# Differential attention on one Trainium2 core: paired score matmuls, the mask through an fp32r identity, and negated scores whose minimum is the bias

## The reference, cut to what matters

```python
def diff_causal_attention(q, k, v, lam):
    # q,k: (B,H,2,S,64); v: (B,H,S,128); lam: scalar
    for j in range(S_ // Q_BLOCK):                    # 8 blocks of 128 queries
        lo, hi = j * Q_BLOCK, (j + 1) * Q_BLOCK
        s = jnp.einsum('bhmqd,bhmkd->bhmqk', q[:, :, :, lo:hi], k[:, :, :, :hi]) * 64 ** -0.5
        mask = jnp.arange(hi)[None, :] <= jnp.arange(lo, hi)[:, None]
        p = jax.nn.softmax(jnp.where(mask, s, -jnp.inf), axis=-1)
        pd = p[:, :, 0] - lam * p[:, :, 1]
        outs.append(jnp.einsum('bhqk,bhkd->bhqd', pd, v[:, :, :hi]))
    return jnp.concatenate(outs, axis=2)
```

## Time and profile before

| | us |
|---|---|
| median of 3 runs | 3958.72 |
| lowest, highest | 3958.52, 3963.06 |
| profiled execution | 3959.2 |
| its span | 3957.3 |
| differential attention in it (481.3 to 652.3) | 171.0 |
| mean granted TensorE clock, share of full | 0.932 |

### The profile page before, as it was taken

How to read it: one execution, slowest core, us unless ns; L and a number is a source line. 1 busy time by engine, 2 the same in 40 slices (tenths; PEclk the granted TensorE clock), 3 DMA queues, 4 the chain that set the end, 5 groups by cost and what they waited for, 6 DMA issues and landing times.

```text
span 3957.3 us, 39477 instructions
## 1 busy us (share of the span) xinstructions
PE 3490.5 (88%) x16470; PEld 2812.1 (71%) x16470; DVE 1314.1 (33%) x1746; ACT 691.2 (17%) x1040; POOL 1209.5 (31%) x1052
## 2 busy tenths in 40 slices
PE   5958998779969899899899999994975789999997
PEld 4657865668848678777688888883764568888886
DVE  4153065022150440222411121125699442222223
ACT  2210144121020540001100000002321211000011
POOL 3102201314413023233334343431441234443431
PEclk9978998889979899999999999996987789999998
DMA  2100100101221001012011111111000111111111
GB/s 111 43 16 27 43 1 22 53 13 52 96 91 43 12 22 64 32 43 85 32 54 43 53 42 53 42 53 59 33 22 21 64 43 43 53 42 53 42 53 42
DMA packets 32651, 179.60 MB, mean 45 GB/s; under 512 B 3728, under 2 KB 6800, under 8 KB 15632
## 3 DMA queue, kind: packets, MB, share of 16 engines
q1 hardware_dynamic: 18864, 137.37, 9.8%
q10 hardware_dynamic: 13664, 40.42, 2.7%
HBM read 163.10 MB, written 14.68 MB: 45 GB/s over the span
## 4 chain that ended last, share of the span: by engine, by line
PE 79%; DVE 15%; ACT 3%; issue 2%; POOL 1%; DMA 0%; DVEq 0%; ACTq 0%; POOLq 0%
PE ps L353 46%; PE ps L382 15%; PE ps L408 5%; DVE c_out L1848 4%; PE ps L1610 2%; PE ps L656 2%; DVE xlo L316 1%; PE ps L278 1%; PE ps L1278 1%; PE ps L1294 1%; PE ps L272 1%; DVE n_sq L310 1%; PE ps L718 1%; PE ps L676 1%; DVE n_acc L261 1%
## 5 line engine op out<-in xcount | busy, mean ns | idle before, releaser
L447 POOL TENSOR_TENSOR whi<-raw,par 128x512 fp32r<-128x512 f32 x131 | 146.8, 1121 | 2642.3 <-PE ps L353 1970.3
L451 POOL TENSOR_TENSOR wlo<-raw,whi 128x512 fp32r<-128x512 f32 x524 | 784.0, 1496 | 41.7
L353 PE MATMUL ps<-xhi,whi 128*128 128x512 f32 x2368 | 742.9, 395 | 49.8 <-DVE xlo L316 33.7
L353 PE MATMUL ps<-xlo,whi 128*128 128x512 f32 x2368 | 735.3, 392 | 0.0
L353 PE MATMUL ps<-xhi,wlo 128*128 128x512 f32 x2368 | 733.7, 391 | 0.0
L353 PEld LDWEIGHTS ps<-xhi,whi 128*128 128x128 f32 x2368 | 446.0, 190 | 160.7 <-issue 32.9
L353 PEld LDWEIGHTS ps<-xlo,whi 128*128 128x128 f32 x2368 | 449.3, 190 | 95.0
L353 PEld LDWEIGHTS ps<-xhi,wlo 128*128 128x128 f32 x2368 | 447.9, 189 | 94.3
L449 POOL CAST whi<-raw 128x512 fp32r<-128x512 f32 x393 | 300.1, 764 | 0.0
L382 PE MATMUL ps<-hidden_lo,whi 128*128 128x512 f32 x864 | 269.1, 393 | 0.0
L382 PE MATMUL ps<-hidden_hi,whi 128*128 128x512 f32 x864 | 268.5, 392 | 0.4 <-DVE hidden_lo L1165 0.4
(11 more groups left out here) (409 smaller groups left out, 4088.4 us busy)
## 6 DMA issues: line engine op xcount, KB each, us to landing
raw<-stream SPq DMA_DIRECT2D x131, 1024.0 KB, 4.7
h_scr<-h ACTq DMA_DIRECT2D x2, 4096.0 KB, 12.1
h<-h_scr ACTq DMA_DIRECT2D x2, 4096.0 KB, 14.9
x_in<-xT ACTq DMA_DIRECT2D x4, 1024.0 KB, 14.6
x_again<-xT ACTq DMA_DIRECT2D x4, 1024.0 KB, 8.0
outT<-h ACTq DMA_DIRECT2D x8, 512.0 KB, 3.0
bias<-bias ACTq DMA_DIRECT2D x1, 2560.0 KB, 18.8
o_scr<-o_staged ACTq DMA_DIRECT2D x2, 1024.0 KB, 5.8
```

The costliest lines, as they stand in the source:

```text
L353: mm = nc.tensor.matmul(ps[:, c0 + c:c0 + c + width], w, x(k, a, width), start=(n == 0 and m == 0), stop=(n == len(ks) - 1 and m == 2))
L447: nc.gpsimd.tensor_tensor(WHI[:, r, t], RAW[:, r, t], one, ALU.mult).then_inc(hi_done, 1)
L451: ins = nc.gpsimd.tensor_tensor(WLO[:, r, t], RAW[:, r, t], WHI[:, r, t].bitcast(F32), ALU.subtract)
```

## The change

The two maps' score matmuls are issued in turn, chunk by chunk, on the two halves of the rows, and both masks come after them. All of it waits once, for both exponentials of the step before. The mask matmul takes fp32r copies of identity and mask, made once by ScalarE in the place of `w_if`, which is no longer needed. Queries are scaled by -1/8 when they are copied, and the mask is negated: PSUM holds negated scores, their minimum is the bias of the exponential, and its scale is -1. Two small products of the combination become one instruction. The buffer of squares is single.

```diff
+            pe.wait_ge(S("mask_ready"), 2)
             for i in range(n_steps + 2):
                 if i < n_steps:
                     h, j = STEPS[i]
+                    n = P * (j + 1)
+                    wait(pe, S("d_exp"), 2 * i)
+                    for c in range(0, n, HALF):
+                        w = min(HALF, n - c)
+                        for m in range(2):
+                            rows = slice(64 * m, 64 * m + 64)
+                            nc.tensor.matmul(ps[:, 2 * BANK * m + c:2 * BANK * m + c + w], QT[rows, h, P * j:P * (j + 1)],
+                                             KD[rows, h, c:c + w], start=True, stop=c + w < n)
                     for m in range(2):
-                        wait(pe, S("d_exp"), 2 * i + m - 1)
-                        rows = slice(64 * m, 64 * m + 64)
-                        n = P * (j + 1)
-                        for c in range(0, n, HALF):
-                            w = min(HALF, n - c)
-                            diag = c + w == n
-                            mm = nc.tensor.matmul(ps[:, 2 * BANK * m + c:2 * BANK * m + c + w], QT[rows, h, P * j:P * (j + 1)],
-                                                  KD[rows, h, c:c + w], start=True, stop=not diag)
-                            if diag:
-                                e = 2 * BANK * m + n - P
-                                mm = nc.tensor.matmul(ps[:, e:e + P], IDENT, par("mask_qk", 0, P), start=False, stop=True)
-                        mm.then_inc(S("d_scores"), 1)
+                        e = 2 * BANK * m + n - P
+                        nc.tensor.matmul(ps[:, e:e + P], IDR[:, :], MKR[:, :], start=False, stop=True).then_inc(S("d_scores"), 1)
...
+            nc.scalar.activation(IDR[:, :], IDENT, ACT.Copy).then_inc(S("mask_ready"), 1)
+            nc.scalar.activation(MKR[:, :], par("mask_qk", 0, P), ACT.Copy, scale=-1.0).then_inc(S("mask_ready"), 1)
+            for name, dst, scale in (("q_d", QT, -SCD), ("k_d", KD, 1.0)):
...
-                                             bias=SM[:, i % 4, 2 + m:3 + m], scale=SCD,
+                                             bias=SM[:, i % 4, 2 + m:3 + m], scale=-1.0,
...
-                    v.step(nc_v.tensor_scalar(SM[:, s % 4, 0:1], SM[:, s % 4, 4:5], LM[:, 2:3], None, ALU.mult))
                     v.wait()
-                    v.step(nc_v.tensor_scalar(SM[:, s % 4, 1:2], SM[:, s % 4, 0:1], SM[:, s % 4, 7:8], None, ALU.mult))
+                    v.step(nc_v.scalar_tensor_tensor(SM[:, s % 4, 1:2], SM[:, s % 4, 4:5], LM[:, 2:3], SM[:, s % 4, 7:8],
+                                                     ALU.mult, ALU.mult))
...
-                        v.step(nc_v.tensor_reduce(SM[:, i % 4, m:m + 1], ps[:, 2 * BANK * m:2 * BANK * m + n], AX, ALU.max))
-                        v.wait()
-                        nc_v.tensor_scalar(SM[:, i % 4, 2 + m:3 + m], SM[:, i % 4, m:m + 1], -SCD, None, ALU.mult)\
+                        nc_v.tensor_reduce(SM[:, i % 4, 2 + m:3 + m], ps[:, 2 * BANK * m:2 * BANK * m + n], AX, ALU.min)\
                             .then_inc(S("d_nm"), 1)
```

More of the change, by code:

```diff
@@ L506, in build @@
             PTD = [at("p_t0", A + 84992, [P, 896]), at("p_t1", A + 80896, [P, T])]
-            OSQ = at("o_squares", X + 65536, [P, 2, P])
+            OSQ = at("o_squares", X + 65536, [P, P])
+            WIF_AT = C + -(-4 * PARAMS["w_if"][0] // 32) * 32
+            IDR = at("identity_r", WIF_AT, [P, P], F32R)
+            MKR = at("mask_r", WIF_AT + 4 * P, [P, P], F32R)
             KM = at("k_mem", A + 49152, [P, H1, MEM])
@@ L799, in act_block1 @@
             act.wait_ge(S("ht_ready"), 2 * H1)
-            for name, dst in (("q_d", QT), ("k_d", KD)):
+            nc.scalar.activation(IDR[:, :], IDENT, ACT.Copy).then_inc(S("mask_ready"), 1)
+            nc.scalar.activation(MKR[:, :], par("mask_qk", 0, P), ACT.Copy, scale=-1.0).then_inc(S("mask_ready"), 1)
+            for name, dst, scale in (("q_d", QT, -SCD), ("k_d", KD, 1.0)):
                 q0 = WH[name][1]
@@ L804, in act_block1 @@
                     act.wait_ge(quad_ready, q + 1)
-                    nc.scalar.activation(dst[:, b, :], half(q, b % 2), ACT.Copy).then_inc(free(q), 1)
+                    nc.scalar.activation(dst[:, b, :], half(q, b % 2), ACT.Copy, scale=scale).then_inc(free(q), 1)
             q0 = WH["v_d"][1]
@@ L831, in act_block1 @@
                     act.wait_ge(S("d_on"), s + 1)
-                    wait(act, S("d_sq"), s - 1)
-                    nc.scalar.activation(OSQ[:, s % 2, :], QT[:, h, P * j:P * (j + 1)], ACT.Square,
+                    wait(act, S("d_sq"), s)
+                    nc.scalar.activation(OSQ[:, :], QT[:, h, P * j:P * (j + 1)], ACT.Square,
                                          accum_out=OS1[:, 0, s:s + 1]).then_inc(S("d_sq"), 1)
```

## The result

| | before | changed |
|---|---|---|
| median, us | 3958.62 | 3934.35 |
| lowest, highest | 3957.56, 3963.06 | 3933.24, 3937.59 |
| runs | 4 | 4 |
| ratio, 95% interval | | 0.9939, 0.9927 to 0.9951 |
| span of the profiled execution | 3957.3 | 3935.7 |

24.3 us faster.

What follows compares the result with a forecast made beforehand. TensorE was taken as the bound, with the whole change in one stage. Gains by head of 10.3 + 3.5 + 3.5 + 5.5 = 22.8 us, less 7 for clock falls, gave 16: 3943 us, range 3935 to 3953.

Steps and rivals of the forecast that it cites:

- What bounds the kernel now: Edited stage, 171.0 us: holds the whole gain or loss; TensorE never waits in its widest step of 6.77 us.
- Scores in turn on two row halves: Score matmuls: a pair of maps costs what one map cost, 0.20 + 0.213k us for k key blocks.
- Rival 4: Score matmuls: the halves do not run together, each step grows by 0.213k, total 3964 to 3990 us; chance 0.03.
- rival 3: Edited stage: the clock stays at 1.2 GHz, 25 us slower, 3984 us; chance 0.06.
- Mask through fp32r: Mask matmuls: 0.11 us each, where two took 0.75 a step with their changes of tile.
- VectorE: Small operations: 64 of 0.154 us go, and 0.46 of 0.56 us is left ahead of each combination.
- The new wait: Both maps wait for both exponentials: a step is 1.28 + 0.588k us, a full-clock head gains 3.5.
- The tiling rule, weighed: Whole stage: TensorE alone would save 12 us a head, some 50 in all; the loop leaves 3.5 a head.
- Head 1, at 1.2 GHz: First head: loop of 1.5 + 0.80k us, clock back at step 5; 45.8 to 35.5 us, gain 10.3.
- Head 4 with tail: Last head and tail: 48.2 to about 42.7 us, gain 5.5, of which 3.5 is the head.
- What the clock takes back: Starts of heads 2 to 4: four to six clock falls of 1.0 to 1.7 us, 7 us; bounds 0 and 13.
- Rival 1: Edited stage: the clock is held and the loop alone sets the time, 3936 us; chance 0.15.

## Why the prediction missed

**What bounds the kernel now**: right. TensorE left no time in a wide step before; the stage held the whole change.

**Scores in turn on two row halves**: right. A pair at k = 8 took 1.92 us (priced 1.90), at k = 1 0.42 (priced 0.41). Rival 4 is out. So is rival 3: the clock is at 1.2 GHz for 17 of the stage's 148.8 us.

**Mask through fp32r**: right, somewhat low. Two masks took 0.27 us to the transposes (priced 0.22), and the reader started 0.36 after the mask (priced 0.31). In fp32 a step is 0.16 longer (0.1 in the text).

**VectorE** and **Copies**: right. 0.45 from reciprocal to combination (priced 0.46).

**The new wait**: right, but for one leg, and the core of the case. Measured 3.65, 4.22, 4.78, 5.34, 5.93 for k = 4 to 8, against 3.63, 4.22, 4.81, 5.40, 5.99. The leg that differs: the chain goes through one minimum and both exponentials, not through two minima and the second exponential. Both paths are ready within 0.03 us of each other in wide steps (618.26 + 1.11 and 617.00 + 2.36), so the forecast of a step came out right although the path was the other one; that is luck in the sizes of the two operations. Steps 1 to 3 measured 4.36, 3.28, 3.10 (4.3, 3.2, 3.3). A head at full clock is 34.65, a gain of 4.0 where 3.5 was priced.

**The tiling rule, weighed**: by TensorE's work alone a head would have lost 12 us. TensorE's busy time did fall by 12.0 (37.5 to 25.5), the head by 4.0. The Trainium skill, TensorEngine Tiling (Array Packing), section Performance Considerations, has it that tiling does not quicken the reading of PSUM. The trace agrees: a minimum over 1024 columns takes 1.22 us as the maximum did, the exponential 1.11 as before, and 20 us of extra TensorE work cost nothing.

**Head 1, at 1.2 GHz**: right. 2.83, 3.20, 3.98, 4.75, then 4.22, 4.78, 5.35, 5.93: 35.0 (priced 35.5). The clock rose 14.3 us in, at the step named.

**Head 4 with tail**: too low. From the same end points 48.16 went to 41.73, a gain of 6.4 where 5.5 was priced. 0.4 is the head; the rest is a fall that the kernel before had in its tail (645.7 to 649.1) and the changed kernel has not. The 0.96 of the earlier trace rows showed it, and the sum left it out. There is one trace of the kernel before, so it stays open whether that fall is in all of its runs.

**What the clock takes back**: this is the step that failed. Its place was right: the only fall stands at the start of a head, and costs 1.5 us, inside the 1.0 to 1.7 named. The count was wrong: one, not four to six, so 1.5 us instead of 7. It came from the mean clocks of two other stages, with the new one put between them by its busy share. That share does not tell the count: heads 2 and 3 of the changed kernel run the same instructions in the same steps, and one fell and the other did not. The kernel with the fp32 mask has a busier TensorE (28.9 of 37.3 us in head 3, against 27.1 of 36.1, each with a fall in it) and fell four times. The bounds of the term were loose too: from 3.3 to 4.0 is 0.7 and not 1.0 us, and a fall in steps 1 to 6 would by the text's own two formulas (a difference of 0.22 + 0.212k a step) cost 5.8 us a head, not 4.2. Neither decided the miss. Rival 1, the clock held, was nearest to what happened and got a chance of 0.15. The range gave this term 0 to 13 us, and with nothing taken back its low end was as low as the sum alone, which was itself 2 us short. That left no room for both.

From 3943 to 3934.35 there are 8.7 us: 5.5 are the count of falls, 2.2 the sum with the clock held (25.0 instead of 22.8: 0.3 to 0.5 in each of heads 1 to 3, 0.9 in head 4 and tail), and the last 1.0 is the difference between the stage's 23.5 and the medians' 24.3, with rounding.

**What stays open**: what decides whether a given head start falls. Between the kernels with one fall and with four, the waits at a head's start differ by 0.1 and 0.3 us. Heads 2, 3 and 4 of the changed kernel have the same waits to 0.01 us, and only head 3 fell. The place within the stage matters (the fall moved to the tail when the starts were filled), and three repeats of the changed kernel agree. No experiment here moved the work in time and left it otherwise alone, which would take that apart. From this trace the count can be bounded, not told.

## What to carry to other kernels

When an edit takes work from the engine that bounds a loop, add up the ring through the other engines first: the new step is that ring, and what stands in it counts in full, however idle its engine looks. On a TensorE that now waits, price the clock as a range of its own, from no fall to one at every pause, and put both ends in the range together with the error of the sum. Time on TensorE that nobody uses can be given to matmuls whose result is thrown away, where a pause stands just before a burst. Look at the whole stage after it: this took 6.4 us off the kernel with the fp32 mask and nothing off the changed one, as its one fall moved; there it took pauses filled from before the stage to its tail, with the second set of buffers, to win 6.6 us of the stage and 4.4 of the median.

## What the runs showed of the hardware

- The clock fell with TensorE partly busy throughout: pauses of 1.45 and 0.92 us around 0.8 us of work were followed by 3.5 us at 1.2 GHz. The Trainium skill, TensorE: Matmul & The Clock Gate, section A second HAM failure mode: psum-queue depth-cycling, tells of a clock that falls and rises where TensorE idles briefly and often between groups of matmuls. The trace agrees that this can happen, and adds that it need not: TensorE waited in 25 steps of the changed kernel, and one fall followed.
- One fall cost 1.5 us at the start of a head (5.84 instead of 4.36) and as much in the tail (last step and tail 15.84 us in the kernel with filled head starts, 14.30 in the changed one).
- In these profiles a small lengthening of steps cost more than itself: 8 us of products in the ring became 17 us of stage, 18 us of reduces became 31, by more falls (six and ten, for one).
- Head 1 in the changed kernel was at 1.2 GHz for 13.6 us; with the 2 us pause ahead of it and those of its first steps filled, not at all. Before the change it was at 1.2 GHz for 27.3 us (481.9 to 509.2), though TensorE was busy for 45.6 of that head's 45.8 us.
- Two fp32 masks cost TensorE 0.75 us with their changes of tile, one map after the other, two fp32r masks 0.42, and in one group behind both maps' scores 0.27.
- Outside the edited stage the same instructions took between 3777.5 and 3790.3 us in the sixteen profiles. A single profile can't show a change of a few microseconds there, so the prediction's test of 3 us for other stages was too narrow.
